# A hybrid backbone's mixer: the triangular block inversions of the two DeltaNet directions placed in different quarters of the TensorE array and issued in turns

## What is computed

```
a_mat = where(strict, einsum('bhnik,bhnjk->bhnij', kb, k) * decay, 0.0)
sol = triangular_solve(a_mat + eye(CHUNK), rhs, left_side=True, lower=True, unit_diagonal=True)
```

## Time and profile before

| | us |
|---|---|
| runs | 2085.33, 2085.83, 2085.99 (median 2085.83) |
| profiled execution, own time | 2086.15 |
| span of its profile | 2084.4 |
| mixer, layer 0 | from about 291.4 to 545 |
| mixer, layer 1 | from about 1323 to 1565 |
| TensorE busy, share of the span (an average over all phases) | 84% |
| records of L1052 on TensorE | 5120 matmul, 5120 weight load |

### The profile page before, as it was taken

The page is one execution under the profiler, slowest core; times in us unless marked ns, Lnnn a source line. Parts: engine busy times, 40 slices in busy tenths (PEclk is TensorE's granted clock), DMA queues, the critical chain, the costliest instruction groups (busy, mean ns, idle before and its releaser), DMA issues. The chain is left out here.

```text
span 2084.4 us, 38031 instructions
## 1 busy us (share of the span) xinstructions
PE 1759.4 (84%) x14245; PEld 1412.7 (68%) x14246; DVE 1295.0 (62%) x1877; ACT 958.7 (46%) x1486; POOL 210.6 (10%) x267
## 2 busy tenths in 40 slices
PE   5499988999699299999974999899996939999992
PEld 0299767888444078888863997788883528888882
DVE  0439645666432399687747495566662369999674
ACT  0134543333311088586643445334332228888661
POOL 0000022222000000000011000222220010000001
PEclk8699999999899599999996999999997969999996
DMA  9631034000457599799752220000004049999954
GB/s 392 244 111 67 18 131 145 3 2 2 133 225 258 217 361 398 281 403 389 288 189 91 88 84 0 13 12 2 3 2 144 31 187 390 402 394 401 360 197 165
DMA packets 96374, 376.48 MB, mean 181 GB/s; under 512 B 14527, under 2 KB 35079, under 8 KB 65527
## 3 DMA queue, kind: packets, MB, share of 16 engines
q1 hardware_dynamic: 80534, 316.76, 40.4%
q0 software_dynamic: 8496, 30.94, 4.0%
q10 hardware_dynamic: 7216, 26.97, 3.2%
HBM read 332.86 MB, written 41.78 MB: 180 GB/s over the span
## 5 line engine op out<-in xcount | busy, mean ns | idle before, releaser
L1931 DVE TENSOR_TENSOR expert_w_lo<-shared,expert_w_hi 128x2048 fp32r<-128x2048 f32 x192 | 430.6, 2286 | 43.6 <-ACT expert_w_hi L1873 43.0
L1873 ACT ACTIVATE expert_w_hi<-shared 128x2048 fp32r<-128x2048 f32 x192 | 361.2, 1916 | 57.8 <-PEq L142 54.2
L1815 PE MATMUL ps<-expert_w_hi,expert_x_hi 128*128 128x512 f32 x592 | 232.3, 392 | 5.1 <-DVE expert_x_lo L1927 5.1
L1817 PE MATMUL ps<-expert_w_hi,expert_x_lo 128*128 128x512 f32 x592 | 231.8, 392 | 0.0
L1816 PE MATMUL ps<-expert_w_lo,expert_x_hi 128*128 128x512 f32 x592 | 231.7, 391 | 0.0
L1815 PEld LDWEIGHTS ps<-expert_w_hi,expert_x_hi 128*128 128x128 f32 x592 | 112.1, 189 | 29.2 <-issue 5.9
L1816 PEld LDWEIGHTS ps<-expert_w_lo,expert_x_hi 128*128 128x128 f32 x592 | 112.1, 189 | 23.3
L1817 PEld LDWEIGHTS ps<-expert_w_hi,expert_x_lo 128*128 128x128 f32 x592 | 112.0, 189 | 23.4
L1851 PE MATMUL ps<-expert_w_hi,expert_hid_hi 128*128 128x512 f32 x296 | 118.6, 401 | 1.0 <-ACT expert_hid_hi L1905 0.3
L1852 PE MATMUL ps<-expert_w_lo,expert_hid_hi 128*128 128x512 f32 x296 | 115.5, 390 | 0.0
L964 POOL TENSOR_TENSOR mixer_NTb<-mixer_Bt,consts_sb 128x256 f32<-128x256 f32 x120 | 89.1, 766 | 228.1 <-DVE mixer_Bt L1234 181.1
(11 more groups left out here) (344 smaller groups left out, 3648.0 us busy)
## 6 DMA issues: line engine op xcount, KB each, us to landing
shared<-in_w_gate SPq DMA_DIRECT2D x64, 1024.0 KB, 6.9
shared<-in_w_up SPq DMA_DIRECT2D x64, 1024.0 KB, 8.7
shared<-in_w_down SPq DMA_DIRECT2D x64, 1024.0 KB, 9.3
setup_m_ada_ring<-in_w_ada SPq DMA_DIRECT2D x24, 1024.0 KB, 10.5
shared<-in_w_in SPq DMA_DIRECT2D x10, 2048.0 KB, 7.8
y_table<-expert_y ACTq DMA_DIRECT2D x37, 512.0 KB, 8.8
y_table<-zero SPq DMA_DIRECT2D x1, 12800.0 KB, 41.0
qkv<-in_w_ada SPq DMA_DIRECT2D x11, 1024.0 KB, 5.0
```

The source lines that it names most:

```text
L1815: pe.matmul(bank, hi, w_hi[:, j, w], start=first, stop=False)
L1817: return pe.matmul(bank, lo, w_hi[:, j, w], start=False, stop=last)
L1873: act.activation(w_hi[:, j, :], raw[:, j, :], ACT.Copy).then_inc(w_hi_done, 1)
L1931: dve.tensor_tensor(w_lo[:, j, :], raw[:, j, :], w_hi[:, j, :].bitcast(F32), ALU.subtract).then_inc(w_lo_done, 1)
```

## The change

Direction 0 stays where it was. For direction 1, Y and T1 of block b now lie on the partitions of the other half (`place`); X, NTb and the results that are used later stay. So x0, t1 and xx of d=1 go through the off-diagonal quarters of the array, while yy of d=1 stays on a diagonal one. Y0 is made in two halves per direction, because input and output partitions differ for d=1.

The order on TensorE is new. x0 of both directions in turns, product by product. Then d=1 lags by half a level: t1 of d=0 at v in turns with xx of d=1 at v-1 (for v=0 and v=5 the one that exists alone), then yy of d=1 at v-1; at v=2 and v=3 the turn and the scores stand here; then xx of d=0 in turns with t1 of d=1 at v, then yy of d=0. In front of each set of products in turns stand the waits of both. ScalarE's and GpSimd's queues are unchanged, VectorE's but for the halves.

```diff
+        def place(d, b):
+            return b if d == 0 else 1 - b
...
-                def eight(b, c, lhsT, rhs, sem):
-                    for h in range(DH):
-                        for r in range(2):
-                            mm = pe.matmul(G.ps[half(r), b, 256 * c + h * HB:256 * c + (h + 1) * HB],
-                                           lhsT(h)[half(r)], rhs(h)[half(r)], start=True, stop=True)
-                    mm.then_inc(s_[sem], 1)
+                def x0(d, h, b):
+                    y = half(place(d, b))
+                    return pe.matmul(G.ps[half(b), d, h * HB:(h + 1) * HB], Y[y, d, h, :], G.c("eye")[y], start=True, stop=True)
+                def t1(v, d, h, b):
+                    return pe.matmul(G.ps[half(place(d, b)), d, h * HB:(h + 1) * HB], NTb[half(b), v % 2, d, h, :], X[half(b), d, h, :],
+                                     start=True, stop=True)
+                def xx(d, h, b):
+                    y = half(place(d, b))
+                    return pe.matmul(G.ps[half(b), d, 256 + h * HB:256 + (h + 1) * HB], Y[y, d, h, :], T1[y, d, h, :],
+                                     start=True, stop=True)
+                def yy(d, h, b):
+                    y = half(place(d, b))
+                    return pe.matmul(G.ps[y, 2 + d, h * HB:(h + 1) * HB], T1[y, d, h, :], Y[y, d, h, :], start=True, stop=True)
+                def wait_t1(s, v, d):
+                    pe.wait_ge(s_["nt_done"], lev(s, v, d))
+                    if v == 0:
+                        pe.wait_ge(s_["x0_done"], at(s, d))
+                    else:
+                        pe.wait_ge(s_["x_done"], lev(s, v - 1, d))
+                def wait_xx(s, v, d):
+                    pe.wait_ge(s_["t1_done"], lev(s, v, d))
+                    if v:
+                        pe.wait_ge(s_["y_done"], lev(s, v - 1, d, LV - 1))
+                    else:
+                        pe.wait_ge(s_["qk_done"], at(s, d))
+                places = [(h, b) for h in range(DH) for b in range(2)]
...
-                    for d in range(2):
-                        pe.wait_ge(s_["y0_done"], at(s, d))
-                        eight(d, 0, lambda h: Y[:, d, h, :], lambda h: G.c("eye"), "x0_p")
+                    pe.wait_ge(s_["y0_done"], at(s, 1))
+                    for h, b in places:
+                        m0 = x0(0, h, b)
+                        m1 = x0(1, h, b)
+                    m0.then_inc(s_["x0_p"], 1)
+                    m1.then_inc(s_["x0_p"], 1)
+                    for v in range(LV + 1):
+                        if v == 0:
+                            wait_t1(s, v, 0)
+                            for h, b in places:
+                                m0 = t1(v, 0, h, b)
+                            m0.then_inc(s_["t1_p"], 1)
+                        elif v < LV:
+                            wait_t1(s, v, 0)
+                            wait_xx(s, v - 1, 1)
+                            for h, b in places:
+                                m0 = t1(v, 0, h, b)
+                                m1 = xx(1, h, b)
+                            m0.then_inc(s_["t1_p"], 1)
+                            m1.then_inc(s_["xx_p"], 1)
+                        else:
+                            wait_xx(s, v - 1, 1)
+                            for h, b in places:
+                                m1 = xx(1, h, b)
+                            m1.then_inc(s_["xx_p"], 1)
+                        if v:
+                            for h, b in places:
+                                m1 = yy(1, h, b)
+                            m1.then_inc(s_["yy_p"], 1)
                         if v == 2:
                             turn(n0)
                         if v == 3:
                             next_scores(n0 + 1)
+                        if v < LV:
+                            wait_xx(s, v, 0)
+                            wait_t1(s, v, 1)
+                            for h, b in places:
+                                m0 = xx(0, h, b)
+                                m1 = t1(v, 1, h, b)
+                            m0.then_inc(s_["xx_p"], 1)
+                            m1.then_inc(s_["t1_p"], 1)
+                            for h, b in places:
+                                m0 = yy(0, h, b)
+                            m0.then_inc(s_["yy_p"], 1)
...
-                        dve.tensor_tensor(Y[:, d], NTb[:, 1, d], row(G.c("eye"), DH), ALU.add).then_inc(s_["y0_done"], 1)
+                        for b in range(2):
+                            ins = dve.tensor_tensor(Y[half(place(d, b)), d], NTb[half(b), 1, d], row(G.c("eye")[half(b)], DH), ALU.add)
+                        ins.then_inc(s_["y0_done"], 1)
...
                                 for b in range(2):
-                                    ins = dve.tensor_tensor(YF[half(b), d, :, half(b)], Y[half(b), d], blocks(2 + d)[half(b)],
-                                                            ALU.subtract)
+                                    y = half(place(d, b))
+                                    ins = dve.tensor_tensor(YF[half(b), d, :, half(b)], Y[y, d], blocks(2 + d)[y], ALU.subtract)
```

## The result

| | before | after |
|---|---|---|
| runs of the comparison | 2085.99 us median (2085.33 to 2087.95, 5 runs) | 2095.1 us median (2093.64 to 2098.75, 5 runs) |
| profiled execution, own time | 2086.15 | 2094.4 |
| span | 2084.4 | 2092.7 |

The ratio after to before is 1.0047, with a 95% interval of 1.0035 to 1.0059: 9 us slower. I had forecast 2087.0, about 1 us slower, and meant by it little or no change (2082 to 2090). The result lies outside that band, though inside the range of 2078 to 2112.

A forecast was written before the change was run, and what follows sets the result against it. Levels were taken as bound by TensorE's issue, other places by waits on VectorE and attention products. Passes and Y0 together gave -1.9 us, the clock +3.2: +1.3 on 2086.15 is 2087.4, less 0.3 for the runs' median: 2087, range 2078 to 2112.

The forecast's parts named there:

- Brackets at 0.47 us: TensorE, t1 of one direction in turns with xx of the other: four quarters run together, 16 products in 0.47 us.
- B0: The bracket of v=0 with xx of direction 0 and t1 of direction 1; any bracket was forecast at 0.47 us.
- rival 3: The nine brackets: quarters don't run together, each takes 0.93 us; +36.5 us, 2122; chance 0.15.
- The pass at full clock: x0 to t1l takes 22.1, 20.6 and 18.2 us at 512, 384 and 128 keys; -0.2 us with 512.
- A's wait: Ahead of a bracket with t1 of direction 0: four semaphore waits cost 0.22 us, between 0.12 and 0.24.
- the norm: VectorE's work that the turn waits for: falls from 2.04 to 1.26 us, as GpSimd no longer runs beside it.
- A2: The bracket of t1 of direction 0 at v=2: 7.01 us from x0's start, 7.30 before.
- Y0 on the path: VectorE ahead of x0: halves cost 1.2 us extra per pass; +1.3 at s=0, +0.25 at s=1, otherwise hidden.
- The clock: TensorE idle before the turn lets the clock fall: two stretches in ten passes at 1.6 us, +3.2.
- Rival 2: The clock falls at most turns: six to nine stretches, +7.7 to +12.5 us, 2094 to 2098; chance 0.15.
- Rivals 1: More gain arrives: Y0's halves cost 0.42 or other waits 0.07, clock holds; -4.7 to -8.8 us, 2077 to 2081; chance 0.22.
- rival 4: Norm stays at 2.04 us because GpSimd still runs beside it: +6.6 us, with the clock 2093; chance 0.05.

The follow-up runs named there:

- e4: The kernel after with direction 1 on the same array quarters as direction 0, all else kept: 2123.52 us (one run).
- e5: The kernel after with direction 0's Y0 written as one instruction over 128 partitions again: 2090.8 us.
- e1: The kernel after with products that nobody reads put into TensorE's idle stretches to keep it busy: 2094.26 us.
- e6: The kernel after with the four semaphore waits ahead of bracket A coded in another order, that for T of direction 1 first: 2092.09 us.
- e7: The kernel after with the first item's transposes moved from ahead of bracket B of level 2 to behind its Y products: 2084.34 us.
- e10: The kernel before with the first item's transposes moved behind the products of level 2: 2075.76 us, ratio 0.9947 to before.
- e3: The kernel before with only Y0 made in two halves per direction, partitions not shifted: 2087.61 us, ratio 1.0007 to before.
- e2: The kernel after with GpSimd starting the masks of level 0 only when both Y0 are done: 2091.14 us.
- e9: The kernel after with the edits of e2, e5, e6 and e7 together, run in more rounds: 2074.35 us, ratio 0.9947 to before.
- e11: The kernel after with each bracket issuing one direction's eight products, then the other's, not in turns: 2108.05 us.

## Why the prediction was right or wrong

- **Brackets at 0.47 us: right.** B0's 32 records go by in 0.46 us. The Trainium skill (TensorE: Matmul & The Clock Gate, Part 3) has loads overlap only where row groups differ; here neighbours on the same rows overlap, and e4 shows what it would cost if not: 2123.5, where rival 3 had 2122. The Trainium skill's floor of about 25 ns from start to start (same page, Part 1) isn't there either: 32 records in 0.46 us are 14 ns each.
- **The pass at full clock: right.** 22.00 us with 512 keys (22.0 to 22.1 forecast), 20.7 with 384 (20.6; e5; the one such pass without a fall in the kernel after took 21.0), 18.4 with 128 (18.2; e1). A's wait of 0.23 against 0.22, the norm (412.15 to 413.42, 1.27 us against 1.26), the turn at 9.66 us from x0 against 9.88 came close to what was worked out; A2 stood at 6.76 against 7.01. In ten passes some 4.7 us gained, 5.0 forecast.
- **Y0 on the path: mis-sized.** I took 1.2 us extra per pass, and its rows gave 1.72 (3.31 less 1.59), above even my upper bound of 1.6, which was itself too low (four of the earlier trace rows's 0.83 less 1.59 is 1.73): all four instructions took 0.82, though GpSimd, as I had it, would be away from one. At s=1 I set 0.96 of slack against it and had +0.25, where it was +0.82; at s=0 +1.83 against +1.3. Over ten passes 5.5 us instead of 3.1.
- **The clock: the step that failed.** I put +3.2 for two stretches at the turn, at 1.6 each. The traces show eleven against three before: seven more inside passes, at 0.7 to 0.9 each where a pass without them is there to compare, and behind t1l two new ones of 1.6 in layer 1 and one fewer in layer 0. The place was wrong too. Only one stood at a turn (behind 511.4, at s=4). Four began 1.4 to 2.2 us behind an x0 at s=0 or 1, after TensorE had waited for Y0 (busy 1.82 and 1.06 of 3.4 us), a fifth followed one of them, and two came late in layer 0's first pass, the first of these behind 3.4 us with TensorE busy 0.47, during its stalls. At the turn with 512 keys the clock held, though TensorE was busy only 1.48 of the 3.4 us that I laid around the wait at 410.0. The step that failed was to take the busy share around one wait, wherever it lay, for a forecast of a fall. Rows that I cut myself and rows that end at a fall aren't the same kind, so they don't show either that the busy share has no part in it. With 512 keys the scores fill the wait for Y0 (2.82 busy around x0 at 402.0), and no fall came there. I had looked for idle only at the turn; the lengthened wait ahead of x0 brought a second one to the start of the pass, so two of my terms were one cause. What is left of 10.1 us in the mixers after -4.7 for the passes, +5.5 for x0 and 0.3 between steps is 9.0, for the clock and the stalls of layer 0's first pass together. For layer 1 e1 bears the clock's part out (5.3); how the clock and the stalls share layer 0's part stays open.
- **Rival 2** came nearest in time (2094 to 2098) and in kind, not in place.
- **Rivals 1 and 4** didn't come: A's wait was 0.23 and not 0.07 (e6 gets most of it back by order), and norm ran alone. Two sums there were off: rival 3's 38 less 1.9 is 36.1, and rival 4's +6.6 with the clock's +3.2 is 2096, not 2093.
- **The range** held the result, but that says little for the mechanism. It was 34 us wide to take in quarters that run partly together, which didn't happen; the result got there by two costs that I had set too low, Y0's and the clock's.
- **What I didn't name**: the turn with ready products behind it. I counted its idle time as given; moving the call was worth 11 us in either kernel (e7, e10), more than the 9 that the change cost.

## What to carry to other kernels

Filling idle parts of the array paid here only where issue was the bound. Ask what the engine waits for once its products are free: here 3.7 us less of busy TensorE in a pass gave 0.3. Move a wait that has ready, independent work behind it before anything is made faster: here that one edit was worth 11 us, where the crossing shortened ten passes by 4.7. And count the length of each half when an instruction is split for the sake of layout: here a half took as long as the whole (0.82 against 0.83 us), which cost time once the next stage waited for all of them (e3 against the kernel after).

## What the hardware did that I had not expected

- A clock fall of 3.4 us at 0.50 costs half as much inside a pass (0.7 to 0.9 us) as behind it (1.6). Inside one, a bracket stretches from 0.46 to 0.81 us while VectorE's copy stays at 0.42.
- VectorE's 64x256 sum of two SBUF operands takes 815 ns on average beside GpSimd's multiplications, 494 where one of a step's four has them beside it (e2), and 420 for the two in e9 that have none. An instruction with an operand in PSUM didn't show this (419 ns).
- Four semaphore waits ahead of a load cost 0.23 us after the late one and 0.15 less in a better order.
- TensorE starts records of the next group among the last four of the one ahead when they are for other quarters (e11), but in the bracket read no earlier.
